# Gate exponential of four forward groups issued one step early, and score products moved in front of the state products

## The chip, the cores and the metric

The kernel runs on one core of a Trainium2 chip. The metric is the device time of one execution in microseconds; the median of three runs is given, and beside it one execution was taken by the hardware profiler, from which all rows come. The engines are named as in the profile: PE (matrix products), PEld (loading of PE's stationary operand), DVE (vector), ACT (activation functions), POOL (general purpose) and SP (which only issues DMAs here).

## What is computed

The reference is a two-layer backbone over 2048 latent tokens and 256 context tokens of width 1024. The change lies in layer 0, a bidirectional gated linear recurrence with 8 heads of width 128. Cut to what matters, for one head and one direction:

```python
f   = lb + (1 - lb) * sigmoid(h @ w_f)         # gate; lf = log(f), k = 1 - f
b_c = cumsum(lf, within a chunk of 64 tokens)
b_mid = b_c at the middle of the chunk
a   = (q * exp(b_c - b_mid)) @ (k * exp(b_mid - b_c)).T     # scores, masked to one triangle
S   = decay * S + k_end.T @ v                  # state, chunk after chunk
o   = (q * exp(b_c)) @ S_prev + a @ v
```

q and the output gate z go through silu. The forward direction scans the context and then the latent tokens; the backward one scans the context and then the latent tokens in reverse. Layer 1 (pooling) and the final norm are not touched by the change.

## The kernel before, in words

**Staging.** One program per engine, tied by counting semaphores. `need(e, name, per, h, c)` (line 325) makes engine `e` wait until semaphore `name` has `h * per + c`. Every engine runs `head(...)` for 8 heads, and in it a loop over 23 steps, `st` = 0 to 22, one for each entry of `GROUPS`: five v groups (steps 0 to 4), four q groups (5 to 8), five f groups of the forward gate (9 to 13, `F0` = 9; the first of them is the context, 256 columns wide, the others are 512 wide), five b groups of the backward gate (14 to 18, again context first) and four z groups (19 to 22). The order of work on each engine is the program order of its loop, written out by hand; `fi = st - F0 - n` picks the gate group that a part of the step works on, n steps behind its projection. `lat(fi)` numbers the eight latent gate groups, `ai` = 0 to 7.

**PE, per step.** The projection of group `st` into one of two PSUM banks: 16 wide products (`wide_parts`, lines 1375 and 1376) and 8 narrow ones (line 1380); up to `AHEAD` = 14 wide and narrow of a group stand together, from there on the wide part of group `st + 1` is put behind the narrow part of `st`. Behind the projection, in this order, for the gate groups: the transposes of the keys of `fi = st - 11` (line 1496, "key turns"; two for the context, else four), the output products of `fi = st - 13` (line 1512, "O", 16 matmuls, and in the backward direction line 1520), the state products of `fi = st - 12` (line 1535, "U", 16 matmuls, 8 for the context), and the scores of `fi = st - 11` (line 1548, "A", 16 small matmuls into one bank). A(ai) waits for `a_masked`, that is until DVE has copied A(ai-1) out of that bank. O waits for `w_step`, the chain of states, all but its last step. U waits for the token-major keys of ACT (`kt_ready`).

**ACT, per gate step.** Line 763: Exp of the projection from PSUM into `xa[st % 2]`. Then (for fi = st - 11 below `KEY_EARLY` = 3) the key copy of line 744; Ln (780), Exp (782), Ln (790, the log gate into `xb`), Identity (795, the key into `kp`); the key copy for later fi; then a small Exp (810, `em`), and the two Exps of lines 813 and 814 of the centred sums. The queue is in order: an instruction whose wait isn't met holds all behind it.

**DVE, per gate step.** The clamp of `xa` (1121), which needs the Exp of line 763; the gate products of the group one step back (1130 to 1144; line 1144 finishes the keys and counts `x_done`, for which the key turns wait); the scan (1158) of this group's log gates, needs line 790; the centring (1165); `advance(h, fi)` (1056, 1058), the state chain of `fi = st - 12`, eight dependent steps (four for a context), which need U; last the masked copy of the scores (1195) of `fi = st - 11`. For fi = 0 the chain stands at the head of step 12, ahead of the clamp.

**POOL.** Line 643 scales the query for the O products (`q2`), behind `o_done` of the O before; lines 617 to 621 split the weights.

The clamp's place in DVE's program is behind the chain and the masked copy of the step in front; lines 617 to 621 and 643 are not edited.

Of the kernel before, what the change touches and what calls it, by code (L numbers as in the profile page):

```python
# [15 lines left out]
ACT = mybir.ActivationFunctionType  # L16
# [10 lines left out]
CHUNK = 64  # L27
# [9 lines left out]
GROUPS = ([("v", "c")] + [("v", b) for b in range(NBLK)] + [("q", b) for b in range(NBLK)]  # L37
          + [("f", "c")] + [("f", b) for b in range(NBLK)]
          + [("b", "c")] + [("b", b) for b in reversed(range(NBLK))]
          + [("z", b) for b in reversed(range(NBLK))])  # L40
NG = len(GROUPS)
# [4 lines left out]
F0 = 9  # L46
X0 = 5
NV = 5
NX = NG - X0
NF = 10  # L50
NA = 8
# [27 lines left out]
def width(blk):  # L79
    return CTX if blk == "c" else BLK  # L80
# [12 lines left out]
AHEAD = 14  # L93
WO_ACT = (2, 3, 6, 7)
KEY_EARLY = 3


def lat(fi):

    return None if fi in (0, 5) else (fi - 1 if fi < 5 else fi - 2)  # L100
# [8 lines left out]
def hybrid_kernel(nc, x, ctx, ada_w, ada_late, vecs, w_in, w_out, pool_w_in, pool_w_grp, pool_w_out,  # L109
# [7 lines left out]
    with es:  # L117
# [22 lines left out]
        bank = [es.enter_context(nc.psum_tensor(f"bank{i}", [P, BLK], FP32)) for i in range(8)]  # L140
        PJ0, PJ1, TB, AB, U0, U1, OB, MB = range(8)
# [40 lines left out]
        kp = place("kp", [P, 3, BLK], FP32)  # L182
# [3 lines left out]
        xa = place("xa", [P, 2, BLK], FP32)  # L186
        xb = place("xb", [P, 2, BLK], FP32)
        qp = place("qp", [P, 2, BLK], FP32)
# [118 lines left out]
        s = {}  # L307
# [17 lines left out]
        def need(e, name, per, h, c):  # L325

            v = h * per + c
            if not isinstance(v, int) or v > 0:
                e.wait_ge(s[name], v)
# [370 lines left out]
        def _(act):  # L700
# [30 lines left out]
            act.wait_ge(s["set_dve"], 5)  # L731
            modulate_first(act, 0)

            def key_copy(h, fi):

                if 0 <= fi < NF:
                    n = 2 if fi in (0, 5) else 4
                    need(act, "kt_tr", NF, h, fi + 1)
                    need(act, "u_done", NF, h, fi - 1)
                    if fi == 0:  # L740
                        need(act, "late_acc", NLATE, h, NLATE)
                    if fi == 1:
                        need(act, "late_mm", 2, h, 2)
                    act.activation(k_tok[:, fi % 2, 0:n, :],
                                   bank[TB][:, 0:n * P].rearrange("p (a b) -> p a b", b=P),
                                   ACT.Copy).then_inc(s["kt_ready"], 1)

            def head(h, first, last):
                for st in range(NG):
                    if first and st < NBLK:  # L750
                        modulate_first(act, st + 1)
                    kind, blk = GROUPS[st]
                    w = width(blk)
                    need(act, "proj_done", NG, h, st + 1)
                    pj = bank[PJ0 + (h * NG + st) % 2]
                    if kind == "v":
                        need(act, "v_tr", NV, h, st)
                        act.activation(v_t[:, 0:w], pj[:, 0:w], ACT.Copy).then_inc(s["proj_read"], 1)
                    else:
                        xi = st - X0  # L760
                        p = xi % 2
                        need(act, "x_done", NX, h, xi - 1)
                        ex = act.activation(xa[:, p, 0:w], pj[:, 0:w], ACT.Exp, scale=-1.0)  # L763
                        if kind in "qz":
                            act.activation(xb[:, p, 0:w], pj[:, 0:w], ACT.Copy).then_inc(s["proj_read"], 1)  # L765
                        else:
                            ex.then_inc(s["proj_read"], 1)
                    if last and st == NG - 1:
                        round_tile(0, 0)
                        round_weights(0, WO_ACT[:2])  # L770
# [1 line left out]
                    if X0 <= st < NG:  # L772
                        xi = st - X0
                        p = xi % 2
                        kind, blk = GROUPS[st]
                        w = width(blk)
                        if st - (F0 + 2) < KEY_EARLY:
                            key_copy(h, st - (F0 + 2))
# [4 lines left out]
                        if kind in "fb":  # L783
                            fi = st - F0
# [8 lines left out]
                            if fi >= 4:  # L793
                                need(act, "a_done", NA, h, sum(lat(i) is not None for i in range(fi - 2)))
                            act.activation(kp[:, fi % 3, 0:w], xa[:, p, 0:w], ACT.Identity,
                                           scale=hv[:, 6 + o // 2:7 + o // 2], bias=hv[:, o + 1:o + 2]
                                           ).then_inc(s["k_ready"], 1)

                    if st - (F0 + 2) >= KEY_EARLY:
                        key_copy(h, st - (F0 + 2))  # L800
                    fi = st - F0
                    if 0 <= fi < NF:
                        p = (fi + 4) % 2
# [18 lines left out]
                    fi = st - (F0 + 4)  # L822
# [54 lines left out]
            for i in range(NTL + 1):  # L877
                if 0 < i < NTL - 1:
                    round_tile(0, i + 1)
                if i < NTL:  # L880
                    t = tile_of(i)
# [18 lines left out]
            for g in range(4):  # L900
                for st in range(4 * NBLK):
# [9 lines left out]
                    pj = bank[PJ0 + st % 2]  # L911
# [460 lines left out]
        def _(pe):  # L1372
# [15 lines left out]
            for n in range(2 * KT):  # L1388
                k, half = n // 2, n % 2
                pe.wait_ge(s["alo_ready"], n + 1)  # L1390
                for part in (ada_hi, ada_lo):
                    for i in range(2):
                        last = pe.matmul(bank[MROW[2 * half + i]][0:4, :], sil4[:, k, :],
                                         part[:, n % 4, i * BLK:(i + 1) * BLK], start=(k == 0 and part is ada_hi),
                                         stop=(k == KT - 1 and part is ada_lo), skip_group_check=True)
                last.then_inc(s["mod_done"], 1)
            for j in range(2 * KT):
                if j % 4 == 0:
                    pe.wait_ge(s["mrow_act" if j < KT else "mrow_dve"], j % KT // 4 + 1)
                last = pe.matmul(bank[TB][:, 2 * j:2 * j + 2], mrow[:, j // KT, j % KT * P:(j % KT + 1) * P],  # L1400
                                 sel[:, :], start=(j == 0), stop=True, skip_group_check=True)
# [56 lines left out]
            def head(h, first, last_head):  # L1458
                for st in range(NG):
# [7 lines left out]
                    if 1 <= st <= NV:  # L1467
# [5 lines left out]
                        for i in range(nt):  # L1473
                            last = pe.transpose(bank[TB][:, i * P:(i + 1) * P], v_t[:, i * P:(i + 1) * P],
                                                ident[:, :])
                        last.then_inc(s["v_tr"], 1)
                    if late_sum_at(st, first) is not None:
# [5 lines left out]
                        for j in range(2):  # L1483
                            last = pe.matmul(bank[MB][:, 2 * half + j:2 * half + j + 1], lacc[:, half, j * P:(j + 1) * P],
                                             one_col[:, :], start=(half == 0 and j == 0), stop=True,
                                             skip_group_check=True)
                        last.then_inc(s["late_mm"], 1)
                    fi = st - (F0 + 2)
                    if 0 <= fi < NF:

                        need(pe, "x_done", NX, h, fi + 5)
                        if fi == 0:
                            need(pe, "v_ready", NV, h, NV)
                        need(pe, "kt_ready", NF, h, fi)
                        for j in range(2 if lat(fi) is None else 4):
                            last = pe.transpose(bank[TB][:, j * P:(j + 1) * P], kp[:, fi % 3, j * P:(j + 1) * P],  # L1496
                                                ident[:, :])
                        last.then_inc(s["kt_tr"], 1)
                    fi = st - (F0 + 4)
                    if 0 <= fi < NF and lat(fi) is not None:  # L1500

                        ai = lat(fi)
# [6 lines left out]
                        for n in range(8):  # L1509
                            c = n if d == 0 else 7 - n  # L1510
                            r = slice(c % 2 * CHUNK, (c % 2 + 1) * CHUNK)
                            last = pe.matmul(o[r, c // 2 * P:(c // 2 + 1) * P],  # L1512
                                             q2[:, ai % 2, c * CHUNK:(c + 1) * CHUNK],
                                             w_st[:, (8 * ai + n) % 16, :], start=(n < 2), stop=(d == 0),
                                             skip_group_check=True)
                        if d == 1:
                            need(pe, "a_summed", 4, h, ai - 3)
                            for c in range(8):
                                r = slice(c % 2 * CHUNK, (c % 2 + 1) * CHUNK)
                                last = pe.matmul(o[r, c // 2 * P:(c // 2 + 1) * P], asum[r, c // 2, :],  # L1520
                                                 v_tok[r, 2 + 4 * b + c // 2, :], start=False, stop=True,
                                                 skip_group_check=True)
                        last.then_inc(s["o_done"], 1)
                    fi = st - (F0 + 3)
                    if 0 <= fi < NF:
# [6 lines left out]
                        for j in range(n):  # L1532
                            for half in range(2):
                                r = slice(half * CHUNK, (half + 1) * CHUNK)
                                last = pe.matmul(bank[U0 + half][:, j * P:(j + 1) * P], k_tok[r, fi % 2, j, :],  # L1535
                                                 v_tok[r, t0 + j, :], start=(j == 0), stop=True,
                                                 skip_group_check=True)
                        last.then_inc(s["u_done"], 1)
                    fi = st - (F0 + 2)
                    if 0 <= fi < NF:  # L1540

                        if lat(fi) is not None:
                            ai = lat(fi)
                            need(pe, "a_masked", NA, h, ai)
                            for c in range(8):
                                r = slice(c % 2 * CHUNK, (c % 2 + 1) * CHUNK)
                                t = slice(c * CHUNK, (c + 1) * CHUNK)
                                last = pe.matmul(bank[AB][r, c // 2 * CHUNK:(c // 2 + 1) * CHUNK], kp[:, fi % 3, t],  # L1548
                                                 qp[:, ai % 2, t], start=(c < 2), stop=True,
                                                 skip_group_check=True)  # L1550
                            last.then_inc(s["a_done"], 1)
                    if st == 1 and not first:
                        turn_out(h, -1)
                    if last_head and st == LATE_OUT - 1:
# [147 lines left out]
```

## Time and profile before

| | us |
|---|---|
| median of 3 runs | 2111.95 (2111.46 to 2112.65) |
| the profiled execution, its own time | 2111.99 |
| its span, first to last instruction | 2110.1 |
| one head, fourth and fifth of eight | 155.6 each |
| PE busy in the span | 2041.7 (97%) |
| DVE, ACT, POOL busy | 1272.3 (60%), 934.5 (44%), 480.2 (23%) |

The eight heads fill the span from about 90 to 1330 us. PE is the busiest engine in every slice of them. A busy share of 97% leaves some 68 us of idle time in the whole span, so a change that removes no matmul can only win from those; where they lie is told by the waits. In the timelines one line is a run of equal instructions: start, time from the first start to the last end, engine, line, operation, tiles and count, and in brackets the idle time of the engine before it and what ended that.

### The profile page before, as it was taken

To read this page: it belongs to the slowest core of one execution; us is meant where nothing else is said; L and a number is where in the kernel's file an instruction comes from. 1 tells how busy PE (TensorE), PEld (TensorE's weight loads), DVE (VectorE), ACT (ScalarE), POOL (GpSimd) and SP (SyncE) were. 2 spreads that over 40 slices of the span, in tenths; PEclk is the share of its full clock that TensorE was granted. 3 is DMA by queue.
4 is the path that set the end of the run, shared out by engine and by line. 5 is a ranking of instruction groups with operands and counts; after the bars stand their busy time and mean duration, and the time that the engine had idled before them with its cause. 6 is when DMAs were issued, how large, how long until landed. Compare 5 with 4: busy or idle time off the path is not lost.

```text
span 2110.1 us, 31949 instructions
## 1 busy us (share of the span) xinstructions
PE 2041.7 (97%) x12322; PEld 1454.3 (69%) x12322; DVE 1272.3 (60%) x2361; ACT 934.5 (44%) x1962; POOL 480.2 (23%) x446
## 2 busy tenths in 40 slices
PE   6799999999999999999999999899999999999998
PEld 3567767777777777777777777677666666666665
DVE  7848648548548558458458467655563546465444
ACT  7746346356356256256256266444413131214222
POOL 2022222222322323313213221100162222200000
PEclk8999999999999999999999999999999999999999
DMA  7210110110110210210110111443221010205443
GB/s 284 94 57 11 48 54 11 59 43 11 61 41 11 66 36 12 65 36 16 61 36 21 60 31 72 154 145 130 100 73 63 23 66 21 90 11 170 142 145 113
DMA packets 106759, 144.55 MB, mean 69 GB/s; under 512 B 7136, under 2 KB 74224, under 8 KB 105584
## 3 DMA queue, kind: packets, MB, share of 16 engines
q1 hardware_dynamic: 99648, 125.72, 18.4%
q10 hardware_dynamic: 6960, 16.80, 2.1%
q8 instruction: 98, 1.61, 0.3%
q14 instruction: 53, 0.43, 0.1%
HBM read 108.91 MB, written 33.57 MB: 68 GB/s over the span
## 4 chain that ended last, share of the span: by engine, by line
PE 80%; ACT 8%; DVE 7%; issue 2%; DMA 2%; POOL 0%; SPq 0%; DVEq 0%; ACTq 0%; POOLq 0%
PE bank L1375 22%; PE bank L1376 22%; PE bank L1380 21%; PE bank L1535 3%; PE bank L1512 3%; PE bank L1621 3%; DVE xb L1158 2%; PE bank L1548 2%; PE bank L1520 1%; ACT xa L780 1%; ACT xa L782 1%; ACT xb L790 1%; PE bank L1496 1%; DVE lacc L1214 1%; DVE xa L1165 1%
## 5 line engine op out<-in xcount | busy, mean ns | idle before, releaser
L1375 PE MATMUL bank<-h_hi,w_hi 128*128 128x512 f32 (+1 forms) x1472 | 575.1, 395 | 0.0
L1376 PE MATMUL bank<-h_hi,w_lo 128*128 128x512 f32 (+1 forms) x1472 | 548.1, 377 | 0.0
L1380 PE MATMUL bank<-h_lo,w_bf 128*128 128x512 bf16 (+1 forms) x1472 | 329.8, 367 | 0.0
L1375 PEld LDWEIGHTS bank<-h_hi,w_hi 128*128 128x128 f32 x1472 | 277.7, 189 | 56.6
L1376 PEld LDWEIGHTS bank<-h_hi,w_lo 128*128 128x128 f32 x1472 | 278.0, 189 | 47.5
L1380 PEld LDWEIGHTS bank<-h_lo,w_bf 128*128 128x128 bf16 x1472 | 131.4, 98 | 145.0 <-issue 25.1
L1058 DVE SCALAR_TENSOR_TENSOR w_st<-w_st,cv,bank 128x128 f32<-128x128 f32 x560 | 194.2, 347 | 23.5
L1375 PE MATMUL bank<-wo_hi,og_hi 128*128 128x512 f32 x496 | 197.5, 398 | 3.1 <-DVE og_lo L1221 2.2
L1376 PE MATMUL bank<-wo_hi,og_lo 128*128 128x512 f32 x496 | 193.4, 390 | 0.0
L643 POOL TENSOR_TENSOR q<-qp,cv 128x512 f32<-128x512 f32 x64 | 80.7, 1262 | 486.7 <-DVE qp L1142 154.4
L617 POOL TENSOR_TENSOR w_hi<-w_raw,zero_col 128x512 fp32r<-128x512 f32 x80 | 91.1, 1138 | 435.3 <-PE bank L1380 241.2
L780 ACT ACTIVATE xa<-xa 128x512 f32<-128x512 f32 (+1 forms) x144 | 87.5, 608 | 178.7 <-DVE xa L1121 178.6
L1375 PE MATMUL bank<-h_hi,pw_hi_b 128*128 128x512 f32 x384 | 162.2, 422 | 0.7 <-POOL pw_lo_b L692 0.7
L1376 PE MATMUL bank<-h_hi,pw_lo_b 128*128 128x512 f32 x384 | 149.9, 390 | 0.0
L1158 DVE TENSOR_TENSOR_SCAN xb<-reset,xb 128x512 f32<-128x512 bf16 (+1 forms) x80 | 98.1, 1226 | 75.0 <-ACT xb L790 75.0
L763 ACT ACTIVATE xa<-bank 128x512 f32<-128x512 f32 (+1 forms) x144 | 81.4, 565 | 131.0 <-PE bank L1380 131.0
L433 ACT ACTIVATE xn<-xr 128x1024 f32<-128x1024 f32 x32 | 33.9, 1061 | 230.6 <-DVE xr L1267 230.6
L1121 DVE TENSOR_SCALAR xa<-xa 128x512 f32<-128x512 f32 (+1 forms) x144 | 79.0, 548 | 87.3 <-ACT xb L765 48.2
L663 POOL CAST og_bf<-og 128x1024 bf16<-128x1024 f32 x30 | 32.2, 1076 | 381.5 <-DMA og<-pooled_scratch 230.4
L621 POOL TENSOR_TENSOR w_lo<-w_raw,w_hi 128x512 fp32r<-128x512 f32 x80 | 115.7, 1446 | 0.0
L1380 PE MATMUL bank<-wo_lo,og_bf 128*128 128x512 bf16 x496 | 112.6, 380 | 0.1
L1375 PEld LDWEIGHTS bank<-wo_hi,og_hi 128*128 128x128 f32 x496 | 93.2, 188 | 24.6 <-DVE og_lo L1221 4.3
(185 smaller groups left out, 3366.3 us busy)
## 6 DMA issues: line engine op xcount, KB each, us to landing
w_raw<-in_w_in SPq DMA_DIRECT2D x80, 256.0 KB, 2.8
ada_sb<-in_ada_w SPq DMA_DIRECT2D x8, 1024.0 KB, 12.2
xt<-in_x SPq DMA_DIRECT2D x16, 512.0 KB, 6.1
ada_a<-in_ada_late SPq DMA_DIRECT2D x64, 128.0 KB, 2.1
ada_b<-in_ada_late SPq DMA_DIRECT2D x64, 128.0 KB, 2.2
gated_scratch<-o_t ACTq DMA_DIRECT2D x32, 256.0 KB, 2.4
xr<-in_x SPq DMA_DIRECT2D x16, 512.0 KB, 4.9
x_scratch<-xr ACTq DMA_DIRECT2D x16, 512.0 KB, 2.9
```

The lines of the kernel that those rows point to most:

```text
L617: pool.tensor_tensor(w_hi[:, b, :, :], raw, zero_col[:, 0:1].unsqueeze(2).to_broadcast([P, 4, P]), ALU.add).then_inc(s["w_part"], 1)
L621: pool.tensor_tensor(w_lo[:, b, :, :], raw, w_hi[:, b, :, :].bitcast(FP32), ALU.subtract).then_inc(s["w_cut"], 1)
L643: pool.tensor_tensor(q2[:, p, :].rearrange("p (c t) -> p c t", t=CHUNK), qp[:, p, :].rearrange("p (c t) -> p c t", t=CHUNK), c.unsqueeze(2 ...
L763: ex = act.activation(xa[:, p, 0:w], pj[:, 0:w], ACT.Exp, scale=-1.0)
L780: act.activation(xa[:, p, 0:w], xa[:, p, 0:w], ACT.Ln, bias=1.0).then_inc(s["ln1p"], 1)
L1058: dve.scalar_tensor_tensor(w_st[:, (at + n + 1) % 16, :], w_st[:, (at + n) % 16, :], cv[:, fi, n:n + 1], u, ALU.mult, ALU.add).then_inc(s[ ...
L1121: dve.tensor_scalar(xa[:, px, 0:w], xa[:, px, 0:w], CLAMP, None, ALU.min).then_inc(s["clamped"], 1)
L1158: dve.tensor_tensor_scan(sums, reset[:, 0:w], sums, 0.0, ALU.mult, ALU.add).then_inc(s["scanned"], 1)
L1375: pe.matmul(out_ap, hi, m_hi, start=start, stop=False)
L1376: pe.matmul(out_ap, lo, m_hi, start=False, stop=False)
L1380: return pe.matmul(out_ap, bf, m_lo, start=False, stop=stop)
L1512: last = pe.matmul(o[r, c // 2 * P:(c // 2 + 1) * P], q2[:, ai % 2, c * CHUNK:(c + 1) * CHUNK], w_st[:, (8 * ai + n) % 16, :], start=(n < ...
```

## The change

`EXP_EARLY` is `range(10, 14)`: the groups of steps 10 to 13, the four 512-wide groups of the forward gate. For these the Exp of line 763, with its waits (`proj_done` of its group and `x_done` of the group two back), is taken out of its own step and put into the step in front, behind the key's Identity (line 795) and ahead of the later key copy and the small Exp of line 810. And the A block (line 1548) of PE moves up inside each step: it stands directly behind the key turns, in front of O and U, in the steps of all eight latent groups. No instruction is added or removed.

```diff
+EXP_EARLY = range(F0 + 1, F0 + 5)
...
+            def gate_exp(h, st):
+
+                xi = st - X0
+                w = width(GROUPS[st][1])
+                need(act, "proj_done", NG, h, st + 1)
+                need(act, "x_done", NX, h, xi - 1)
+                act.activation(xa[:, xi % 2, 0:w], bank[PJ0 + (h * NG + st) % 2][:, 0:w], ACT.Exp, scale=-1.0
+                               ).then_inc(s["proj_read"], 1)
+
...
-                    need(act, "proj_done", NG, h, st + 1)
+                    if st not in EXP_EARLY:
+                        need(act, "proj_done", NG, h, st + 1)
...
-                    else:
+                    elif kind in "qz":
...
-                        ex = act.activation(xa[:, p, 0:w], pj[:, 0:w], ACT.Exp, scale=-1.0)
-                        if kind in "qz":
-                            act.activation(xb[:, p, 0:w], pj[:, 0:w], ACT.Copy).then_inc(s["proj_read"], 1)
-                        else:
-                            ex.then_inc(s["proj_read"], 1)
+                        act.activation(xa[:, p, 0:w], pj[:, 0:w], ACT.Exp, scale=-1.0)
+                        act.activation(xb[:, p, 0:w], pj[:, 0:w], ACT.Copy).then_inc(s["proj_read"], 1)
+                    elif st not in EXP_EARLY:
+                        gate_exp(h, st)
...
+                    if st + 1 in EXP_EARLY:
+                        gate_exp(h, st + 1)
                     if st - (F0 + 2) >= KEY_EARLY:
                         key_copy(h, st - (F0 + 2))
...
                         last.then_inc(s["kt_tr"], 1)
+                    fi = st - (F0 + 2)
+                    if 0 <= fi < NF:
+
+                        if lat(fi) is not None:
+                            ai = lat(fi)
+                            need(pe, "a_masked", NA, h, ai)
+                            for c in range(8):
+                                r = slice(c % 2 * CHUNK, (c % 2 + 1) * CHUNK)
+                                t = slice(c * CHUNK, (c + 1) * CHUNK)
+                                last = pe.matmul(bank[AB][r, c // 2 * CHUNK:(c // 2 + 1) * CHUNK], kp[:, fi % 3, t],
+                                                 qp[:, ai % 2, t], start=(c < 2), stop=True,
+                                                 skip_group_check=True)
+                            last.then_inc(s["a_done"], 1)
                     fi = st - (F0 + 4)
...
                         last.then_inc(s["u_done"], 1)
-                    fi = st - (F0 + 2)
-                    if 0 <= fi < NF:
...
-                            last.then_inc(s["a_done"], 1)
```

## Rows read from the trace of the kernel before

**Rows 1.** The page, busy time of PE over the span.
```profile
PE 2041.7 (97%) x12322; PEld 1454.3 (69%) x12322; DVE 1272.3 (60%) x2361; ACT 934.5 (44%) x1962; POOL 480.2 (23%) x446
```

**Rows 2.** Waits of PE in the span: total us, times, longest us.
```profile
PE bank L1512 <- issue: 6.9, 8, 0.9
...
PE bank L1548 <- DVE am L1195: 4.3, 8, 0.5
PE bank L1496 <- DVE kp L1144: 3.3, 5, 1.5
```

**Rows 3.** Timeline of PE, fourth head, steps 12 to 15, without the wide products.
```profile
621.41 0.66 PE L1496 MATMUL bank<-ident,kp 128*128 128x128 f32 x4
622.00 0.72 PE L1535 MATMUL bank<-v_tok,k_tok 64*128 64x128 f32 x8
622.64 0.69 PE L1548 MATMUL bank<-qp,kp 128*64 128x64 f32 x16
627.03 1.90 PE L1380 MATMUL bank<-h_lo,w_bf 128*128 128x512 bf16 x8
...
629.30 1.16 PE L1535 MATMUL bank<-v_tok,k_tok 64*128 64x128 f32 x16
631.00 0.69 PE L1548 MATMUL bank<-qp,kp 128*64 128x64 f32 x16 [0.54 <-DVE am L1195]
...
638.18 0.60 PE L1496 MATMUL bank<-ident,kp 128*128 128x128 f32 x4
639.68 1.09 PE L1512 MATMUL bank<-w_st,q 128*64 128x128 f32 x16 [0.90 <-issue]
...
641.79 0.69 PE L1548 MATMUL bank<-qp,kp 128*64 128x64 f32 x16
642.41 1.90 PE L1380 MATMUL bank<-h_lo,w_bf 128*128 128x512 bf16 x8
647.83 0.60 PE L1496 MATMUL bank<-ident,kp 128*128 128x128 f32 x4
```

**Rows 4.** Timeline of ACT, fourth head, steps 11 and 12.
```profile
619.85 0.63 ACT L780 ACTIVATE xa<-xa 128x512 f32<-128x512 f32 x1 [0.22 <-DVE xa L1121]
...
624.71 0.61 ACT L814 ACTIVATE xa<-xa 128x512 f32<-128x512 f32 x1
625.23 0.58 ACT L763 ACTIVATE xa<-bank 128x512 f32<-128x512 f32 x1
625.71 0.59 ACT L744 ACTIVATE k_tok<-bank 128x512 f32<-128x512 f32 x1
626.30 0.63 ACT L780 ACTIVATE xa<-xa 128x512 f32<-128x512 f32 x1
...
628.35 0.80 ACT L795 ACTIVATE kp<-xa,hv 128x512 f32<-128x512 f32 x1
```

**Rows 5.** Timeline of DVE, fourth head, steps 11 to 13.
```profile
620.67 0.68 DVE L1144 TENSOR_TENSOR kp<-kp,xa 128x512 f32<-128x512 f32 x1
...
625.84 0.43 DVE L1121 TENSOR_SCALAR xa<-xa 128x512 f32<-128x512 f32 x1 [0.35 <-ACT xa L763]
...
628.54 1.25 DVE L1158 TENSOR_TENSOR_SCAN xb<-reset,xb 128x512 f32<-128x512 bf16 x1 [0.73 <-ACT xb L790]
...
630.51 0.43 DVE L1195 COPY_PREDICATED am<-mask,bank 128x256 f32<-128x256 uint8 x1
...
636.93 3.12 DVE L1058 SCALAR_TENSOR_TENSOR w_st<-w_st,cv,bank 128x128 f32<-128x128 f32 x8
639.98 0.44 DVE L1195 COPY_PREDICATED am<-mask,bank 128x256 f32<-128x256 uint8 x1
```

**Rows 6.** Timeline of POOL and DVE, fourth head, step 14.
```profile
640.95 1.43 POOL L643 TENSOR_TENSOR q<-qp,cv 128x512 f32<-128x512 f32 x1 [12.23 <-DVE cv L1136]
...
641.39 1.53 DVE L1144 TENSOR_TENSOR kp<-kp,xa 128x512 f32<-128x512 f32 x1
...
648.01 0.44 DVE L1195 COPY_PREDICATED am<-mask,bank 128x256 f32<-128x256 uint8 x1
```

More of the change, by code:

```diff
@@ L1538, in head @@
                         last.then_inc(s["u_done"], 1)
-                    fi = st - (F0 + 2)
-                    if 0 <= fi < NF:
[L1542 to L1550, printed above, removed]
-                            last.then_inc(s["a_done"], 1)
                     if st == 1 and not first:
```

## Prediction

> **What bounds the kernel now.** I read the busy shares first: PE is at work for 97% of the span [rows 1]. No matmul is removed, so only PE's idle time can be won, and the second view, PE's waits, says which of it the change can reach [rows 2]: in each of the eight heads PE stands still once before A (0.5 us, for the masked copy of the scores before), once before O (0.9 us), and in some heads before the key turns (3.3 us in all, for DVE's key product). That is 4.3 + 6.9 + 3.3 = 14.5 us. The third view, PE's timeline of one head, places them [rows 3]: A(1) of step 13 at 631.00, O of step 14 at 639.68. The row calls the second releaser "issue"; the O block waits for seven of the eight steps of DVE's state chain, which starts at 636.93 with 3.12 / 8 = 0.39 us a step [rows 5], so the seventh ends at 639.66. It is the chain. From step 15 on PE never waits.
>
> The fourth view, ACT's and DVE's timelines, says why both come late. The Ln of one step starts at 619.85 and the next at 626.30 [rows 4]: 6.45 us a step in steps 11 to 13. It is a loop through both engines: Ln, Exp, Ln on ACT, scan and centring on DVE, the two Exps on ACT, then the next group's Exp (625.23), DVE's clamp (625.84 to 626.27), and Ln again. PE had finished that projection long before. The loop is what is late, not PE.
>
> **The change, part by part.** I use the fourth head and count from the start T of its key turns in step 12 (621.41).
>
> *Early Exp.* It costs its 0.48 us of issue in either place (625.23 to 625.71, [rows 4]). In the new place ACT is idle, waiting for the scan, and the clamp can run while ACT does its last two Exps. Where nothing else binds, the next Ln starts right behind ACT's last Exp (0.52 us after its start, 624.71 to 625.23) or behind the key copy (at most 0.59 us). In step 10 that is 1.1 us earlier (625.23 to 626.30, which fall away), in step 11 about 1.9 us (twice that, less 0.3 for the context's short key copy, which was hidden). It brings DVE's key product forward by 1.4 us or more, so the waits before the key turns go, but not wholly in the first head: there the clamp of step 10 stands behind late conditioning pieces that wait for DMAs, and I leave about half of its 1.5 us. Measured as the delay of the turns and not as idle time the head shown gives 0.3, and I take 2.7 us for all heads; bounds 0 and 3.3.
>
> *A in front, step 12.* Before, U starts at T + 0.59 and A at T + 1.23, next work at T + 1.85. Now A starts at T + 0.53 and takes 0.62 (641.79 to 642.41), so U ends at T + 1.86 (its eight take 0.72). DVE's chain of the context now waits for that U: it starts at T + 1.9, where DVE itself would be free at about T + 0.9 (Ln to the end of the centring is 626.30 to 630.51, and Ln(11) comes 1.9 us before 619.85). The clamp of step 12 is behind that chain. Four chain steps take 1.35, the clamp 0.43: Ln(12) starts at T + 3.72, before at T + 4.89. So 1.2 us is left of the 1.9.
>
> *Step 13.* Ln to the end of the masked copy is 626.30 to 630.94, 4.64 us [rows 4, 5]. Now it ends at T + 8.36. A(1) now stands where U(1) stood (629.30, less 0.07), at T + 7.82, and waits to T + 8.42: 0.6 us. Before it waited 0.54 behind U. The copy comes 1.2 us earlier, but A is also asked for 1.1 us earlier: of the wait before A nothing is won. A and U then take 1.7, and PE goes on at T + 10.12, before at T + 10.20.
>
> *The Exp's own wait.* In step 12 ACT is ready for the Exp of group 13 at 3.72 + 2.05 (Ln to Identity) + 0.72 = T + 6.49, but PE ends that projection at 627.03 + 1.90, T + 7.45 with the 0.07. Behind the waiting Exp stand the small Exp and the two Exps of the centred sums, and DVE's key product waits for these. The Exp then ends with the small one at T + 8.17, and the two could have begun at T + 8.04: 0.15 to 0.2 us lost. With it and 0.49 for the key copy Ln(13) starts at T + 9.76, before at T + 11.34.
>
> *Step 14.* From Ln(13) to the end of the next masked copy it was 7.67 us (6.45 behind 626.30, to 640.42 [rows 4, 5]), so the copy ends at T + 17.43 and A(2) starts at T + 17.49; its place on PE, 0.53 behind the turns at 638.18, is T + 17.22. A short wait of 0.3 in place of O's 0.9. A, O and U end 0.61 + 2.11 (639.68 to 641.79) later, at T + 20.21; before at T + 21.00 (642.41). With the small waits a little worse in heads that start earlier, 0.75 us a head: 6.0 us. The bounds of the term: minus 0.8 a head if the copy comes no earlier at all, plus 1.4 if it never binds.
>
> *Steps 15 to 20.* A(3) is wanted at 647.83 + 0.53 - 0.75 = 647.61, and the copy of A(2) ended at 648.45 [rows 3, 6]; it must come 0.9 us earlier, and DVE is ahead by 1.55 us. In the backward steps DVE has gone ahead of PE already, and both gaps grow or stay. The moved A makes O and what DVE adds behind it 0.6 us later, which lies inside DVE's idle time. I cost these at nothing; if DVE's lead were gone, A(3) would pay up to 0.8 us a head. No DMA is moved, and SP's queue is as before.
>
> *Sum.* 8 x 0.75 + 2.7 = 8.7 us off the profiled execution's 2111.99 us (1.9 over its span, 0.04 over the median of the runs): **2103.3 us**.
>
> POOL works from 640.95 on [rows 6], and a key product of DVE that takes 0.68 us elsewhere [rows 5] takes 1.53 beside it. POOL starts when the first O ends, and A now delays O, so POOL starts only 0.1 to 0.45 us earlier while DVE is 1.55 earlier; DVE's product then runs ahead of it, and the scan and centring meet it. The Trainium skill (SBUF — State Buffer, "Who interferes with whom") says that DVE and GpSimd share a port pair, that a DVE instruction with two SBUF inputs contends with a GpSimd one that reads SBUF, and that the second to issue blocks wholly. The stretched row agrees with it. By that rule taken at its worst DVE's lead is tied to POOL's, which is the rival below.
>
> **The rivals.** *All of it is won*: neither A(1) nor A(2) waits, as where the chain in step 12 isn't held by U. 0.54 + 0.90 a head and 2.9 us: 2111.99 - 14.4 = 2097.6. For it: ACT and DVE have the spare time. Against it: the A in front of U, and A's bank, freed only behind the whole chain.
>
> *The lead is lost in step 14* to the shared port: POOL leads by 0.1 to 0.45 only, so the copy of A(2) ends at about 648.2 and A(3) waits 0.6 to 0.8 us. 8.7 less 8 x 0.75 is 2.7: about 2109.3. For it the 1.53 us row; against it that DVE is in front of POOL at the start.
>
> *Slower*: the move of A costs more than the early Exp gives. Its place is A(2) in step 14. Had the masked copy stayed at 640.42, A would start at 640.48 and the block end at 643.20, 0.8 us later than 642.41; 8 x 0.8 = 6.4, so 2118.4. It decides once the copy comes less than 0.8 us earlier; I find 1.55. It would need the early Exp to be held by PE for over 0.7 us more than I find, in step 11 or 12.
>
> *Nothing*: the loop isn't shortened, since the clamp stays behind chain and copy, and the move costs nothing: 2112.
>
> **How the numbers follow.** Forecast, 2099.5 to 2106.5: 0.60. All won: 0.12. Lead lost: 0.14. Nothing: 0.07. Slower: 0.07. A measurement of this kernel tells 0.2%, 4.2 us, from no change. Faster by more: 0.60 + 0.12 + half of the lost lead; within: the other half and the nothing; slower 0.07. The range runs from the all-won case to the lost lead, 2097.5 to 2109.5; outside are the last two and a little of the ends.
>
> **What would show it.** Right: Ln(11), Ln(12), Ln(13) earlier by 1.9, 1.2 and 1.6 us against T; a wait before A in step 13 of about 0.6 us and one before A in step 14 of 0.3, none before O; the waits before the key turns mostly gone; a head 0.75 to 1.6 us shorter; PE's busy time unchanged. Wrong: A in step 13 without a wait (then U did not hold the chain), a wait before A in step 15 (the port), ACT idle before line 763 by more than 1 us, or heads longer than 155.6 us.

## The result, and the profile after

The changed kernel takes 2097.93 us (median of 4 runs, 2097.45 to 2099.03) against 2111.7 us for the kernel before in the same runs: ratio 0.9935, 95% interval 0.9920 to 0.9951. It is 13.8 us faster. The profiled execution took 2098.1 us with a span of 2096.1, 14.0 less than before. The forecast was 2103.3 with a range of 2097.5 to 2109.5: the right side, inside the range, but close to its lower end, with 5.4 us more gain than the sum had.

Work on the engines is the same, as it must be. On the page after, PE's row, to be held against [rows 1]:

```profile
PE 2036.8 (97%) x12322; PEld 1453.3 (69%) x12322; DVE 1278.2 (61%) x2361; ACT 932.6 (44%) x1962; POOL 471.7 (23%) x446
```

The waits of PE after (total us, times, longest). Line 1520 is A, 1537 is O, 1560 is U, 1508 the key turns; they answer to [rows 2]:

```profile
PE bank L1520 <- DVE am L1207: 6.5, 15, 1.2
...
PE bank L1508 <- DVE kp L1156: 1.0, 2, 0.6
...
PE bank L1537 <- issue: 0.5, 1, 0.5
```

14.5 us have become 8.0. So waits explain 6.5 us of the 14.0, less than half of what was gained: most of the rest is in matmuls that follow each other more closely. I call the time from the first start of one block to the first start of the next the block's pitch, and the place where two blocks meet a border. PE's own busy sum says the same, 4.9 us less for equal work.

The timeline of PE after, fourth head, steps 12 to 15, without wide products; it answers to [rows 3]:

```profile
615.33 0.60 PE L1508 MATMUL bank<-ident,kp 128*128 128x128 f32 x4
615.86 0.69 PE L1520 MATMUL bank<-qp,kp 128*64 128x64 f32 x16
616.47 0.71 PE L1560 MATMUL bank<-v_tok,k_tok 64*128 64x128 f32 x8
...
623.74 0.69 PE L1520 MATMUL bank<-qp,kp 128*64 128x64 f32 x16 [0.51 <-DVE am L1207]
624.36 1.16 PE L1560 MATMUL bank<-v_tok,k_tok 64*128 64x128 f32 x16
...
632.02 0.60 PE L1508 MATMUL bank<-ident,kp 128*128 128x128 f32 x4
632.86 0.69 PE L1520 MATMUL bank<-qp,kp 128*64 128x64 f32 x16 [0.24 <-DVE am L1207]
633.37 1.05 PE L1537 MATMUL bank<-w_st,q 128*64 128x128 f32 x16
634.35 1.16 PE L1560 MATMUL bank<-v_tok,k_tok 64*128 64x128 f32 x16
635.44 1.90 PE L1392 MATMUL bank<-h_lo,w_bf 128*128 128x512 bf16 x8
640.85 0.60 PE L1508 MATMUL bank<-ident,kp 128*128 128x128 f32 x4
641.38 0.69 PE L1520 MATMUL bank<-qp,kp 128*64 128x64 f32 x16
641.90 1.05 PE L1537 MATMUL bank<-w_st,q 128*64 128x128 f32 x16
642.87 1.16 PE L1560 MATMUL bank<-v_tok,k_tok 64*128 64x128 f32 x16
643.97 1.90 PE L1392 MATMUL bank<-h_lo,w_bf 128*128 128x512 bf16 x8
```

Read it in two ways. The waits: A in step 13 waits 0.51 us, A in step 14 waits 0.24, O never; the forecast said 0.6 and 0.3. The pitch: step 15 has no wait before or after the change, yet from the key turns to the next narrow products it takes 643.97 - 640.85 = 3.12 us. Before the change it took 3.26, from the turns at 647.83 [rows 3] to the narrow products at 651.09:

```profile
648.36 1.09 PE L1512 MATMUL bank<-w_st,q 128*64 128x128 f32 x16
649.38 1.16 PE L1535 MATMUL bank<-v_tok,k_tok 64*128 64x128 f32 x16
650.48 0.69 PE L1548 MATMUL bank<-qp,kp 128*64 128x64 f32 x16
651.09 1.90 PE L1380 MATMUL bank<-h_lo,w_bf 128*128 128x512 bf16 x8
```

A to O is 0.52 where A to what follows it was 0.61, and O to U 0.97 where it was 1.02.

ACT and DVE after, fourth head. The first Ln of a step is line 790 here (780 before the change), and the gate Exp, now in a function of its own, is line 741. On DVE the chain is lines 1068 and 1070, the key product 1156, the masked copy 1207. First the Ln rows of steps 11 to 13 with the early Exp of group 13, then the start of DVE's chain in step 12:

```profile
612.57 0.62 ACT L790 ACTIVATE xa<-xa 128x512 f32<-128x512 f32 x1
...
619.05 0.63 ACT L790 ACTIVATE xa<-xa 128x512 f32<-128x512 f32 x1 [0.53 <-DVE xa L1133]
...
622.83 0.60 ACT L741 ACTIVATE xa<-bank 128x512 f32<-128x512 f32 x1 [0.93 <-PE bank L1392]
623.33 0.21 ACT L822 ACTIVATE em<-xb 128x8 f32<-128x8 f32 x1
...
625.16 0.62 ACT L790 ACTIVATE xa<-xa 128x512 f32<-128x512 f32 x1
```
```profile
617.23 0.29 DVE L1068 COPY w_st<-bank 128x128 f32<-128x128 f32 x1 [0.39 <-PE bank L1560]
```

Against the key turns of step 12 (615.33) Ln(12) starts at 3.72 us and Ln(13) at 9.83; the forecast had 3.72 and 9.76. DVE waits for U before the chain of step 12, and ACT waits 0.93 us for PE's projection of group 13.

### The profile page after: what moved, and what is told of

Same layout as the page of the kernel before. It is cut to its first block, busy times and chain, and to the rows that moved or that the text cites. A ratio compares the mean times of both kernels' runs of the same rounds, so it can differ in the third digit from the quotient of the medians.

```text
span 2096.1 us, 31949 instructions
## 1 busy us (share of the span) xinstructions
PE 2036.8 (97%) x12322; PEld 1453.3 (69%) x12322; DVE 1278.2 (61%) x2361; ACT 932.6 (44%) x1962; POOL 471.7 (23%) x446
## 4 chain that ended last, share of the span: by engine, by line
PE 87%; DVE 5%; ACT 4%; DMA 2%; issue 2%; POOL 0%; SPq 0%; DVEq 0%; ACTq 0%; POOLq 0%
PE bank L1387 24%; PE bank L1388 24%; PE bank L1392 23%; PE bank L1560 3%; PE bank L1537 3%; PE bank L1633 3%; PE bank L1520 2%; PE bank L1545 2%; PE bank L1508 1%; DVE w_st L1070 1%; DMA ada_sb<-in_ada_w 1%; PE bank L1467 1%; PE bank L1486 1%; ACT hf L477 1%; DVE wo_lo L1256 1%
## 5 line engine op out<-in xcount | busy, mean ns | idle before, releaser
L644 POOL TENSOR_TENSOR q<-qp,cv 128x512 f32<-128x512 f32 x64 | 74.6, 1166 | 485.7 <-PE bank L1537 170.1
L1133 DVE TENSOR_SCALAR xa<-xa 128x512 f32<-128x512 f32 (+1 forms) x144 | 84.0, 583 | 51.0 <-ACT xb L775 48.0
L1113 DVE COPY v_tok<-bank 128x512 f32<-128x512 f32 (+1 forms) x40 | 25.5, 638 | 137.1 <-PE bank L1486 137.0
```

The source lines that it names most:

```text
L644: pool.tensor_tensor(q2[:, p, :].rearrange("p (c t) -> p c t", t=CHUNK), qp[:, p, :].rearrange("p (c t) -> p c t", t=CHUNK), c.unsqueeze(2 ...
L1133: dve.tensor_scalar(xa[:, px, 0:w], xa[:, px, 0:w], CLAMP, None, ALU.min).then_inc(s["clamped"], 1)
```

## The experiments

Theory 1: two separate gains. The early Exp shortens the loop and takes waits away; and wherever A stands directly in front of O, PE needs 0.14 us less for the same matmuls. Theory 2, the rival: the order of the blocks costs nothing in itself, and all of the gain is waits, so the waits left before A are pure loss. In all kernels below the whole computation is kept. Each was timed in one job with the kernel before, whose medians were 2111.9 us (e1 to e4) and 2112.1 us (e5 to e9). The edits are shown against the changed kernel. "scores" stands for the A block, put into a function; in the rows of these kernels it is line 1481, the key turns are 1524, O is 1540 or 1542, U is 1563 or 1565.

**e1_exp_only.** Early Exp, A behind U.

```diff
-                            need(pe, "a_masked", NA, h, ai)
...
-                            last.then_inc(s["a_done"], 1)
                     fi = st - (F0 + 4)
...
                         last.then_inc(s["u_done"], 1)
+                    if True:
+                        scores(h, st)
```

> Early Exp as in the change, A behind U as before. Theory 1 (two gains: shorter waits, and 0.14 us for every step in which A stands directly in front of O, 5 steps a head, 5.6 us in all): the waits of PE before A (0.54 a head) and before O (0.90 a head) and nearly 3 us before the key turns all go, the 0.14 does not come: 2111.9 - 14.4 = about 2097.5, equal to the changed kernel, by another route. Theory 2 (the order of the blocks costs PE nothing in itself, all of the 13.9 us are waits): without the 6.5 us that A waits in the changed kernel, about 2091.4.

Measured: 2097.09 us (ratio 0.9931, 0.9919 to 0.9944). The early Exp by itself gives all that the whole change gives. Of PE's waits before A and before O one of 0.5 us is left in the whole span, and before the key turns one of 0.4. Theory 2 asked for 2091.4, 5.7 us less than was measured.

**e2_move_only.** A in front, no Exp early.

```diff
-EXP_EARLY = range(F0 + 1, F0 + 5)
+EXP_EARLY = ()
```

> A in front of O and U in all steps, no Exp early. Theory 1: A in step 13 waits 1.6 us and PE is 1.05 late, in step 14 A starts behind the masked copy at 640.5 instead of O at 639.7 and the block ends 0.65 us later than before, then 4 steps give back 0.14 each: +0.07 us a head, about 2112.5. Theory 2: nothing is given back, 0.8 x 8 = 6.4 us slower, about 2118.

Measured: 2112.18 us (ratio 1.0002, 0.9993 to 1.0011). Its timeline, fourth head, steps 13 to 15:

```profile
630.45 0.69 PE L1481 MATMUL bank<-qp,kp 128*64 128x64 f32 x16 [1.63 <-DVE am L1207]
...
639.91 0.69 PE L1481 MATMUL bank<-qp,kp 128*64 128x64 f32 x16 [0.61 <-DVE am L1207]
640.43 1.05 PE L1542 MATMUL bank<-w_st,q 128*64 128x128 f32 x16
...
648.43 0.69 PE L1481 MATMUL bank<-qp,kp 128*64 128x64 f32 x16
648.95 1.05 PE L1542 MATMUL bank<-w_st,q 128*64 128x128 f32 x16
```

A waits 17.9 us in all, more than the 14.5 of all the waits before, and still nothing is lost: the closer pitch pays it back. The forecast's "slower" rival priced this order at 2118.4; its waits are there and its sum is not, for the same reason that the forecast was short.

**e3_front_from_15.** Early Exp; A directly behind the key turns only where it need not wait, from step 15 on, else behind U.

```diff
+                    if st >= F0 + 6:
+                        scores(h, st)
...
+                    if st < F0 + 6:
+                        scores(h, st)
```

> Early Exp; A in front only from step 15 on, behind U in steps 12 to 14, where it waits in the changed kernel. Theory 1: the waits go as with the early Exp alone (14.4 us) and 4 steps x 8 heads x 0.14 = 4.5 us come on top: about 2093.0, no wait of PE before A or O. Theory 2: as the early Exp alone, 2091.4.

Measured: 2094.02 us (ratio 0.9915, 0.9902 to 0.9929), 3.1 us below e1 in the same job, and 1.0 above the expectation of theory 1. 32 borders at 0.14 are 4.5 us; in step 15 of the fourth head A starts 0.68 us behind the turns (637.42 to 638.10) in place of 0.53, since the masked copy of A(2) ends only at 638.05, and that takes 1.2 of them back.

**e4_o_a_u.** Early Exp; from step 14 on A between O and U.

```diff
+                    if st >= F0 + 5:
+                        scores(h, st)
...
+                    if st < F0 + 5:
+                        scores(h, st)
```

> Early Exp; from step 14 on A stands between O and U, in steps 12 and 13 behind U. Theory 1a (A and O gain by being neighbours, whichever is first): the waits go and 5 steps x 8 x 0.14 = 5.6 us too, about 2092. Theory 1b (only the first O behind A starts earlier, its stationary operand being loaded under A): 2097.5. Theory 2: 2091.4.

Measured: 2093.99 us (ratio 0.9916, 0.9902 to 0.9929). That lies between the two halves of theory 1, and the timeline says why; steps 15 and 19 of the fourth head:

```profile
640.46 1.09 PE L1540 MATMUL bank<-w_st,q 128*64 128x128 f32 x16
641.39 0.63 PE L1481 MATMUL bank<-qp,kp 128*64 128x64 f32 x16
641.95 1.16 PE L1565 MATMUL bank<-v_tok,k_tok 64*128 64x128 f32 x16
...
672.51 1.09 PE L1540 MATMUL bank<-w_st,q 128*64 128x128 f32 x16
673.53 1.09 PE L1548 MATMUL bank<-v_tok,asum 64*64 64x128 f32 x16
674.55 0.69 PE L1481 MATMUL bank<-qp,kp 128*64 128x64 f32 x16
675.17 1.16 PE L1565 MATMUL bank<-v_tok,k_tok 64*128 64x128 f32 x16
```

In step 15 O to A takes 0.93 and A to U 0.56, together 1.49 where 1.02 + 0.61 were: the gain comes in this order too. In the backward steps the products of line 1548 stand between O and A, and O, 1548 and A keep 1.02, 1.02 and 0.62. So the gain belongs to A and O being neighbours, in either order. Three steps of five have it here, where the expectation of 2092 had counted five: 8 x 3 x 0.14 = 3.4 us below e1, and 3.1 were measured.

**e5_behind_u_in_12.** The changed kernel, but A behind U in step 12, to free DVE's chain there.

```diff
-                            last.then_inc(s["a_done"], 1)
+                    if st != F0 + 3:
+                        scores(h, st)
...
+                    if st == F0 + 3:
+                        scores(h, st)
```

> The changed kernel, but in step 12 A stands behind U as before. If the chain through step 12 is held by U and nothing else, Ln(12) comes 0.5 us earlier against the key turns of its step and A(1), A(2) stop waiting: about 6 us faster than the changed kernel, 2092. If from step 13 on it is the early Exp that waits for PE's projection of group 13 (the hold of the forecast), Ln(12) comes 0.5 us earlier all the same, the wait before A in step 13 goes to about 0.1, ACT waits 1.4 us before the Exp of group 13 in place of 0.9, Ln(13) stays at 9.8 us behind the turns of step 12, and the wait before A in step 14 grows from 0.24 to 0.75: 2098, no change against the changed kernel.

Measured: 2097.66 us (ratio 0.9932, 0.9919 to 0.9944), no change, the second reading. ACT and PE of the fourth head (key turns of step 12 at 614.47):

```profile
617.58 0.63 ACT L790 ACTIVATE xa<-xa 128x512 f32<-128x512 f32 x1 [0.28 <-DVE xa L1133]
621.98 0.60 ACT L741 ACTIVATE xa<-bank 128x512 f32<-128x512 f32 x1 [1.55 <-PE bank L1392]
...
624.31 0.62 ACT L790 ACTIVATE xa<-xa 128x512 f32<-128x512 f32 x1
```
```profile
622.31 0.69 PE L1481 MATMUL bank<-qp,kp 128*64 128x64 f32 x16
...
632.01 0.69 PE L1481 MATMUL bank<-qp,kp 128*64 128x64 f32 x16 [0.83 <-DVE am L1207]
```

Ln(12) starts 3.11 us behind the turns instead of 3.72, but ACT then stands 1.55 us before the Exp of group 13 instead of 0.93, Ln(13) starts at 9.84 as before (9.83), and the wait that A no longer has in step 13 it has in step 14, 0.83 for 0.51 + 0.24. From step 13 on the loop is tied to PE's projection of group 13.

**e6_three_early.** The changed kernel, the Exp of group 13 back in its own step.

```diff
-EXP_EARLY = range(F0 + 1, F0 + 5)
+EXP_EARLY = range(F0 + 1, F0 + 4)
```

> The changed kernel with three groups early (steps 10 to 12), the Exp of group 13 in its own step. The hold on ACT in step 12 goes (0.24 us), but the clamp of group 13 comes after the two Exps: Ln(13) 0.34 us later, A in step 14 waits 0.6 in place of 0.24: 8 x 0.34 = 2.7 us slower than the changed kernel, about 2100.7. If the hold costs more than I think: faster than 2098.

Measured: 2100.38 us (ratio 0.9943, 0.993 to 0.9957), 2.7 us above e5 in the same job, against 2.7 expected over the changed kernel. Measured by what each gained on the kernel before, it is 2.0 us above the changed kernel (11.7 for 13.8). In the fourth head the turns of step 12 to those of step 15 take 25.87 us (615.73 to 641.60), 0.35 more than in the changed kernel, and A waits in step 14:

```profile
633.61 0.69 PE L1481 MATMUL bank<-qp,kp 128*64 128x64 f32 x16 [0.60 <-DVE am L1207]
```

So an Exp that waits early in ACT's queue, and holds what is behind it, is cheaper than a clamp that comes late. The run gives the two together; what the hold costs by itself it doesn't show.

**e9_front_15_no_exp.** The order alone: behind the key turns from step 15 on, else behind U, and no Exp early.

```diff
-EXP_EARLY = range(F0 + 1, F0 + 5)
+EXP_EARLY = ()
...
+                    if st >= F0 + 6:
+                        scores(h, st)
...
+                    if st < F0 + 6:
+                        scores(h, st)
```

> No Exp early; A in front of O and U from step 15 on only, so that the waits of steps 12 to 14 stay as in the kernel before. What is left is the order on PE by itself. Theory 1 (0.14 us a step where A stands directly in front of O, steps 15, 17, 19, 20): 4 x 8 x 0.14 = 4.5 us, less a wait of 0.15 us before A in step 15 (1.2): 2107.4 to 2108.6. Theory 2 (order free): 2112 to 2113.

Measured: 2108.92 us (ratio 0.9985, 0.9977 to 0.9994). That is 0.3 above the expectation of theory 1 and 3 below that of theory 2. Its waits of PE before O and before A are those of the kernel before:

```profile
PE bank L1542 <- issue: 6.9, 8, 0.9
PE bank L1481 <- DVE am L1207: 4.3, 8, 0.6
```

Faster by 3.2 us (1.3 to 4.9 by the interval) with the waits before O and before A as they were. Its profiled execution also waits 1.1 us less before the key turns (2.2 against 3.3), but nothing comes of that: the first head, which had the longest of these waits, reaches its turns of step 12 at 153.70 us in both kernels. The gain is where the order differs. In the fourth head the turns of step 15 to those of step 20 take 41.79 us (646.49 to 688.28), and before the change 42.08 (647.83 to 689.91). With e1, e2 and e3, and the pitch in every timeline, the order has a price of its own, and theory 2 falls.

**e8_best.** Early Exp; A behind U in steps 12 and 13, between O and U in 14 and 15, in front of O from step 16 on.

```diff
+                    if st >= F0 + 7:
+                        scores(h, st)
...
+                    if F0 + 5 <= st < F0 + 7:
+                        scores(h, st)
...
+                    if st < F0 + 5:
+                        scores(h, st)
```

> Early Exp; steps 12 and 13 with A behind U, steps 14 and 15 with A between O and U, from step 16 on A in front of O. Theory 1: the 14.4 us of waits and 5 x 8 x 0.14 = 5.6 us: 2111.9 - 20.0 = 2091.9. Theory 2 (order free): as the early Exp alone, 2097.

Measured: 2092.01 us (ratio 0.9903, 0.9890 to 0.9917), 20.1 us below the kernel before and 6 below the changed one, whose interval it doesn't touch. Both gains are taken whole. A doesn't appear among PE's waits, O has 0.8 us in all, and the key turns have this:

```profile
PE bank L1524 <- DVE kp L1156: 1.0, 2, 0.7
```

## Why the prediction was right, and where it fell short

*What bounds it, and the loop through ACT and DVE*: right. The early Exp shortens the loop; Ln(12) and Ln(13) came where the sum put them, to 0.1 us, and e1 shows that the early Exp by itself was worth 14.8 us, for the 14.5 of waits counted ahead. Ln(11) came 1.2 us earlier against the turns (2.76 us before them, 1.56 before the change) and not 1.9: 0.3 of that is the turns' own move, and 0.4 that the context group's Ln began that much later in this head (11.9 us before the turns, 12.6 before the change). It cost nothing, since U held the chain anyway.

*A in front, step 12*: right. DVE waits for U before its chain. That it is the chain's bound in step 12 alone, and PE's projection of group 13 from there on, is what e5 shows; the forecast had both, and did not say that they cover each other.

*Step 13*: right. 0.51 us of wait for 0.6; nothing was won there.

*The Exp's own wait*: right in size; ACT waited 0.93 us for the 0.96 in the forecast. e6 shows that leaving the Exp of group 13 in its own step, which takes the hold away, costs about 0.34 us a head more.

*Step 14*: here the sum had a term of the wrong size. The wait before A came out (0.24 for 0.3), but "A, O and U end 0.61 + 2.11 later" was mis-sized: the three took 635.44 - 632.86 = 2.58 us, not 2.72. I had given each block the pitch that it had beside its old neighbour, and the new border of A and O costs 0.14 us less.

*Steps 15 to 20, "I cost these at nothing"*: the same error four times more. The delay of O and the waits before A were indeed nothing, and so was the shared port: the copy of A(2) ended at 640.26 + 0.45 = 640.71, A(3) was wanted at 641.38 and didn't wait. But steps 15, 17, 19 and 20 each became 0.12 to 0.18 us shorter: from the step's own narrow products to those of the next it was 8.68, 8.23, 9.69 and 10.17 us before the change and 8.53, 8.08, 9.51 and 10.05 after.

With 5 x 8 x 0.145 = 5.8 us the sum of 8.7 becomes 14.5; 13.9 was measured between the profiled executions. The rest lies mainly in the first head: up to the turns of step 15 it gained 0.7 us (179.44 for 180.15), where the sum had given it the 0.75 of every head and a part of the wait before its turns. It reached the turns of step 11 later (146.98 for 146.40), and those of step 12 still wait, 0.63 us for 1.46 before, as forecast in kind.

Two of the signs named ahead missed for the same reason. A head was to be 0.75 to 1.6 us shorter, and the fourth is 1.84 shorter (153.80 us, 615.33 to 769.13, for 155.64). PE's busy time was to stay the same, and it fell by 4.9 us. That the time still lies inside the range is in part luck: the lower end of the range, 2097.5, came from a rival whose mechanism did not happen, and the term that brought the time there was not in the forecast.

*The rivals.* "All of it is won" gave 2097.6 and is what the clock shows, but by another road: its mechanism, no wait before A, is absent from the changed kernel and present in e1. The lost lead in step 14 did not happen, though DVE was slowed there while POOL worked: the scan of the context group at 634.62 took 1.57 us and the centring 1.01, where those of the other context group (605.07 and 605.87), with the same shapes, took 0.69 and 0.43. The slower rival's condition, a masked copy less than 0.8 us earlier, is met in e2; its loss was paid back by 0.14 in five steps of each head. That a sum lands near a rival's number proves nothing about the rival.

## What to carry to other kernels

When a block of matmuls is moved, cost its borders anew, the ones it leaves and the ones it makes, even where no wait is near; a row without idle time before and after can still change its pitch. When two edits come together, time each alone: here one gave all of the gain, the other added waits and gave back as much in pitch, and only the split showed which steps should have which order. And where a wait goes away in one step, look for the next thing that the same loop waits for: freeing it in step 12 was worth nothing while step 13 was held.

## What the runs showed of the hardware

The gap in loading the stationary operand depends on which blocks are neighbours. PEld of the kernel before, step 15 of the fourth head (lines 1512 O, 1535 U, 1548 A), and then of the changed kernel (1520 A, 1537 O, 1560 U):

```profile
648.36 0.85 PEld L1512 LDWEIGHTS bank<-w_st,q 128*64 128x64 f32 x16 [0.17 <-issue]
649.38 0.97 PEld L1535 LDWEIGHTS bank<-v_tok,k_tok 64*128 64x128 f32 x16 [0.17 <-issue]
650.47 0.55 PEld L1548 LDWEIGHTS bank<-qp,kp 128*64 128x64 f32 x16
```
```profile
641.38 0.55 PEld L1520 LDWEIGHTS bank<-qp,kp 128*64 128x64 f32 x16 [0.17 <-issue]
641.84 0.86 PEld L1537 LDWEIGHTS bank<-w_st,q 128*64 128x64 f32 x16
642.87 0.97 PEld L1560 LDWEIGHTS bank<-v_tok,k_tok 64*128 64x128 f32 x16 [0.17 <-issue]
```

After the turns, and from O to U, the loads stand still for 0.17 us; from U to A it is 0.12 (649.38 + 0.97 = 650.35, to 650.47). Between A and O they do not: the first load for O starts at 641.84, 0.06 us before O's first product, while A's products run to 641.38 + 0.69 = 642.07 by the ends that the profile models. Both blocks have the form 128*64, all rows and half the columns, and within each of them the two halves of the columns take turns (the code's `r`). The products of line 1548 in e4 (64*64) and U (64*128) use half the rows, and no gain appears beside them. One might think that the load slips in because A's last products hold the other half of the columns. The backward steps speak against it. There O takes its parts in reverse (`c = 7 - n`), so that in the program's order it begins with the half with which A ends, and A to O is 0.51 all the same, here in step 19 of the changed kernel:

```profile
673.46 0.69 PE L1520 MATMUL bank<-qp,kp 128*64 128x64 f32 x16
673.97 1.05 PE L1537 MATMUL bank<-w_st,q 128*64 128x128 f32 x16
```

So the order of the halves doesn't decide it. What A and O share is the form 128*64; among the blocks behind the projection no other two neighbours have the same form. That this is the cause is argued and not shown: only the neighbours were varied, not the forms.

The Trainium skill (TensorE: Matmul & The Clock Gate, "The mechanism" under packing) says that loads overlap with matmuls in flight only when the row group differs. Here A and O use the same rows, and the loads of O start 0.06 us before its first product, beside products of A still in flight; their being neighbours saves 0.14 us in this trace. The measurement decides.
